# Zero products spread ahead of and between the first block's steps, and the two experts' weights computed behind the picks, in a two-part transformer kernel

## The reference

```python
def _hier_moe(h, w_group, b_group, w_expert, b_expert, w_gate, w_up, w_down):
    g_prob = jax.nn.softmax(hf @ w_group, axis=-1)
    g_sel = jnp.argmax(g_prob + b_group, axis=-1)
    g_w = jnp.take_along_axis(g_prob, g_sel[:, None], axis=-1)
    e_logits = (hf @ w_expert).reshape(T, MOE_GROUPS, MOE_EXPERTS_PER_GROUP)
    e_prob = jax.nn.softmax(jnp.take_along_axis(e_logits, g_sel[:, None, None], axis=1)[:, 0], axis=-1)
    ...
    _, top_idx = lax.top_k(e_prob + e_bias, MOE_TOP_K)
    top_w = jnp.take_along_axis(e_prob, top_idx, axis=-1)
    top_w = top_w / jnp.sum(top_w, axis=-1, keepdims=True) * g_w
    ...
    def expert_block(args):
        xb, e = args
        return (jax.nn.silu(xb @ w_gate[e]) * (xb @ w_up[e])) @ w_down[e]
    ...
    return jax.ops.segment_sum(yp[dest] * w_s[:, None], tok_s, num_segments=T)
```

## Time and profile before

| | |
|---|---|
| median of three runs | 2360.21 us (2356.59 to 2367.82) |
| the profiled execution's own time | 2359.6 us |
| its span, from the first to the last instruction | 2357.8 us |
| PE busy | 2065.4 us (88%) |
| DVE busy | 1169.1 us (50%) |
| ACT busy | 824.2 us (35%) |
| MoE 0: logits kept by DVE, to the end of its last block | 241.3 to about 693 us |
| MoE 1: logits kept by DVE | 816.9 us |
| mean granted PE clock | 0.948 |

### The profile page before, as it was taken

The page is one execution under the profiler, slowest core; times in us unless marked ns, Lnnn a source line. Parts: engine busy times, 40 slices in busy tenths (PEclk is TensorE's granted clock), DMA queues, the critical chain, the costliest instruction groups (busy, mean ns, idle before and its releaser), DMA issues.

```text
span 2357.8 us, 47090 instructions
## 1 busy us (share of the span) xinstructions
PE 2065.4 (88%) x17804; PEld 1568.1 (67%) x17805; DVE 1169.1 (50%) x2331; ACT 824.2 (35%) x1618; POOL 25.9 (1%) x40
## 2 busy tenths in 40 slices
PE   7999888677779988676678999989999999999997
PEld 3567555344449855343445888877887888877886
DVE  4677422111126632111115666766667766766666
ACT  2232211011125411111114554545555554545554
POOL 0000000000000000000000000000001000100001
PEclk9999999888889999888899999999999999999999
DMA  9978799999996689999998645353555546343552
GB/s 392 339 289 350 325 430 431 431 431 431 431 421 249 236 360 431 431 431 431 431 431 339 202 139 184 108 175 111 169 153 195 183 151 207 108 142 109 197 154 79
DMA packets 273333, 662.59 MB, mean 281 GB/s; under 512 B 6065, under 2 KB 200625, under 8 KB 248113
## 3 DMA queue, kind: packets, MB, share of 16 engines
q1 hardware_dynamic: 273056, 658.82, 72.0%
q10 hardware_dynamic: 144, 2.03, 0.2%
HBM read 659.78 MB, written 1.05 MB: 280 GB/s over the span
## 4 chain that ended last, share of the span: by engine, by line
PE 68%; DMA 19%; DVE 5%; issue 3%; SPq 2%; ACT 1%; another core or an unknown queue 1%; DVEq 0%; ACTq 0%; PEldq 0%
PE ps L2178 20%; PE ps L2183 11%; DMA ring<-in_moe_w_up 8%; DMA A<-in_moe_w_up 8%; PE ps L1582 8%; PE ps L2452 4%; PE ps L1611 3%; DMA arena<-in_moe_w_up 2%; PE ps L2617 2%; PE ps L1564 2%; PE ps L1530 1%; PE ps L1981 1%; PE ps L1983 1%; PE ps L1982 1%; SPq L3007 1%
## 5 line engine op out<-in xcount | busy, mean ns | idle before, releaser
L2178 PE MATMUL ps<-XS,WS 128*128 128x512 f32 x1408 | 502.0, 401 | 8.4 <-DVE XS L691 7.5
L2163 DVE TENSOR_TENSOR WS<-ring,WS 128x1024 fp32r<-128x1024 f32 (+1 forms) x276 | 329.4, 1194 | 227.9 <-ACT WS L2158 227.3
L2158 ACT CAST WS<-ring 128x1024 fp32r<-128x1024 f32 (+1 forms) x276 | 282.8, 1025 | 331.5 <-PE ps L2183 314.1
L2183 PE MATMUL ps<-XS,WS 128*128 128x256 f32 x1408 | 396.2, 281 | 0.0
L1855 DVE TENSOR_TENSOR RS<-RS,ps 64x256 f32<-64x256 f32 x70 | 29.6, 423 | 595.2 <-ACT RS L1676 595.2
L2178 PEld LDWEIGHTS ps<-XS,WS 128*128 128x128 f32 x1408 | 266.6, 189 | 80.2 <-DVE XS L691 17.8
L1582 PE MATMUL ps<-ring,RS 128*32 128x256 f32 x2176 | 236.6, 446 | 86.0 <-DMA ring<-in_moe_w_up 31.8
L2183 PEld LDWEIGHTS ps<-XS,WS 128*128 128x128 f32 x1408 | 268.3, 191 | 0.2 <-issue 0.2
L1582 PEld LDWEIGHTS ps<-ring,RS 128*32 128x32 f32 x2176 | 125.5, 127 | 148.4 <-issue 126.7
L2178 PE MATMUL ps<-HS,WS 128*128 128x512 f32 x616 | 216.4, 396 | 0.0
L1582 PE MATMUL ps<-arena,RS 128*32 128x256 f32 x1120 | 163.2, 456 | 53.7 <-DMA A<-in_moe_w_up 27.5
(11 more groups left out here) (360 smaller groups left out, 3318.3 us busy)
## 6 DMA issues: line engine op xcount, KB each, us to landing
ring<-in_ffn_w_gu SPq DMA_DIRECT2D x90, 1024.0 KB, 7.5
arena<-in_moe_w_down SPq DMA_DIRECT2D x32, 2048.0 KB, 47.7
ring<-in_moe_w_up SPq DMA_DIRECT2D x32, 2048.0 KB, 46.4
ring<-in_moe_w_down SPq DMA_DIRECT2D x32, 2048.0 KB, 46.7
ring<-in_moe_w_gate SPq DMA_DIRECT2D x32, 2048.0 KB, 45.9
ring<-in_w_mod SPq DMA_DIRECT2D x24, 2048.0 KB, 11.9
ring<-in_ffn_w_down SPq DMA_DIRECT2D x32, 1408.0 KB, 6.5
SPARE<-in_moe_w_gate SPq DMA_DIRECT2D x16, 2048.0 KB, 43.2
```

The source lines that it names most:

```text
L2158: L.inc(L.eng.copy(self.parts(u)[0], source), self.w_high)
L2163: L.inc(L.eng.tensor_tensor(wl, self.unit(u)[1], high(wh), ALU.subtract), self.w_split)
L2178: L.eng.matmul(ps[:, bank, :].rearrange("p (j t) -> p j t", j=2), wh[:, i, :], moving[:, :, k, :], start=k == 0, stop=False)
L2183: mm = L.eng.matmul(ps[:, bank, 0:TL], wl[:, i, :], moving[:, 0, k, :], start=False, stop=k == total - 1)
```

## The change

The zero products are no longer in a row. Those of banks 1 and 4 stand ahead of PE's wait for `picks`, that of bank 5 stands behind `pick_block`, and that of bank 6 behind `turn_block`. The wait for the zeros themselves (`y_kept`, a memset by GpSimd) moves ahead of the first two. On DVE the eleven instructions of the weights `WT` move from ahead of the wait for `counts` to behind `picks`, the shift and `ranges`, just ahead of the twelve instructions for `places`. Nothing is added or taken out.

```diff
--- before.py
+++ after.py
@@ -1537,14 +1537,20 @@
                     mm.then_inc(self.block_turned.sem, 1)
 
                 zeros = self.YS.bitcast(BF16)
+
+                def clear(bank):
+                    pe.matmul(ps[:, bank, :], zeros[:, 0:P], zeros[:, 0:512], start=True, stop=False)
+
                 L.wait(self.rows_kept, NT)
+                pe.wait_ge(self.y_kept.sem, 1)
+                clear(1)
+                clear(4)
                 pe.wait_ge(self.picks.sem, 1)
                 pick_block()
-                pe.wait_ge(self.y_kept.sem, 1)
-                for bank in (1, 4, 5, 6):
-                    pe.matmul(ps[:, bank, :], zeros[:, 0:P], zeros[:, 0:512], start=True, stop=False)
+                clear(5)
                 pe.wait_ge(self.picked_kept.sem, 1)
                 turn_block()
+                clear(6)
 
                 for t in range(NT):
                     for c in range(2):
@@ -1767,14 +1773,6 @@
                 step(v.tensor_tensor(by_all(self.BOTH), of_group(self.CE), group4, ALU.mult), self.chosen)
                 for c in range(2):
                     L.inc(v.tensor_tensor(by_all(self.O32S[:, c]), of_group(self.OE[c]), group4, ALU.mult))
-                pick(self.GW, self.GP, self.OG, GROUPS)
-                for c in range(2):
-                    pick(self.WT[c], self.ES, self.OE[c], PER_GROUP)
-                step(v.tensor_tensor(self.WS, self.WT[0], self.WT[1], ALU.add))
-                step(v.reciprocal(self.WS, self.WS))
-                step(v.tensor_tensor(self.WS, self.WS, self.GW, ALU.mult))
-                for c in range(2):
-                    step(v.tensor_tensor(self.WT[c], self.WT[c], self.WS, ALU.mult))
 
                 L.wait(self.counts, 1)
                 over = self.CNT[0:EXPERTS, 0:limits]
@@ -1823,6 +1821,14 @@
                 pick_matched().then_inc(self.picks.sem, 1)
                 L.inc(shift())
                 L.inc(v.tensor_copy(self.FIRSTI, self.FIRST), self.ranges)
+                pick(self.GW, self.GP, self.OG, GROUPS)
+                for c in range(2):
+                    pick(self.WT[c], self.ES, self.OE[c], PER_GROUP)
+                step(v.tensor_tensor(self.WS, self.WT[0], self.WT[1], ALU.add))
+                step(v.reciprocal(self.WS, self.WS))
+                step(v.tensor_tensor(self.WS, self.WS, self.GW, ALU.mult))
+                for c in range(2):
+                    step(v.tensor_tensor(self.WT[c], self.WT[c], self.WS, ALU.mult))
 
                 def lane_of(ap, c, t):
                     return ap[:, NT * c + t:NT * c + t + 1]
```

## The result

The changed kernel takes 2365.05 us in the median of 22 runs (2354.45 to 2370.94), the kernel before 2358.56 us in 22 runs. The ratio is 1.0021 with a 95% interval of 1.0013 to 1.0029: 5 us slower by the ratio, on which this text goes, and 6.5 us by the two medians. That is within 0.5% as forecast, but on the other side of no change, and the median lies above the range that was given (up to 2364 us). The prediction held that 12 us would be needed to tell a change from none; with 22 runs each the interval is 4 us wide. The profiled execution has a span of 2366.6 us, before 2357.8.

What follows compares the result with a forecast made beforehand. The prediction took the DMA queue as full from the restart of the loads to each MoE stage's end. Gains of 1.2 and 1.5 us made 2360.2 - 2.7 = 2357.5 us, range 2357.5 less 6 and up to 2364.

Steps and rivals of the forecast that it cites:

- The weights off the path to the picks: DVE ahead of the picks: the counts' reader starts earlier, gaining 1.30 us in MoE 0 and 1.33 in MoE 1.
- The weights put back behind the picks: DVE between `ranges` and `places`: `places` and all behind come 0.89 us later in MoE 0, 0.86 in MoE 1.
- The zero products: PE ahead of the picks: two products fill the 0.71 us wait, exceed it by 0.22; picks start 1.08 us earlier.
- The step that failed: PE from picks through turn and table: first expert starts 1.4 us earlier in MoE 0, 1.9 in MoE 1.
- the slow rival: PE's clock stays low into the first expert because of short waits: about 2366 us; chance 0.07 for 2362 to 2366.
- the covering load: SP in MoE 1: load behind the table comes 1.5 us earlier, next issue falls inside that load's 4.9 us.
- The way through the full queue: DMA from the loads' restart to stage end: an earlier restart brings the end forward by as much.
- the first rival: Gain lost in the DMA-bound part, up to 2.7 us per stage: 2360 us; chance 0.16 for gain swallowed or halved.
- The sum: Both MoE stages: 1.2 us gained in MoE 0, 1.5 in MoE 1, together 2.7, from 1.8 to 3.5.

Runs made afterwards that it cites:

- second profile of the same kernel: The changed kernel run once more, with nothing altered, beside the kernel before: 2363.9 us, ratio 1.0012.
- extra pair of loads: Kernel before plus one more pair of register loads of the block bounds on PE, ahead of the expert loop: 2361.8 us, ratio 0.9999.
- three products: Changed kernel plus three products of zeros behind the block table on PE: 2359.33 us, ratio 1.0000.
- filled: Changed kernel plus eight products of zeros into PSUM bank 2 behind the block table on PE: 2357.58 us, ratio 0.9996.
- weights in waits: Changed kernel with the group's weight pick moved into the softmax's wait and two experts' picks ahead of the wait for counts: 2356.14 us, ratio 0.9995.
- weights behind alone: Kernel before with only DVE's weights moved behind the picks, the four zero products left in a row: 2361.0 us, ratio 1.0007.

## Why the prediction was wrong, point by point

**The weights off the path to the picks: right.** 1.30 us forecast, 1.34 measured, with a DVE wait of 0.77 us for the counts.

**The weights put back behind the picks: right as to DVE.** The last `places` came 0.87 us later, forecast 0.89; the table's copy and SP's load behind it 1.1 us earlier in MoE 0 (forecast 1.0) and 1.65 in MoE 1 (forecast 1.5).

**The zero products: right, and partly lucky.** The forecast had PE at the low clock there. In the first profile it was at the full clock, so the first two products took 0.59 us, all inside PE's wait, and the picks on PE started 1.43 us earlier, forecast 1.08. In the second profile of the same kernel, where the clock was low at that place, they started 1.26 us earlier.

**The step that failed** is the end of the next one: "One of them takes 1.32 / 4 = 0.33 us", and "The first expert starts at 259.9 us instead of 261.34". I took the end of the table on the array for the start of the expert, as the earlier trace rows show it before: 261.34 for both. What lies between the two in PE's instruction stream, the head of the loop, two register loads and their waits, was put at nothing. It stands in none of the rows that I had read: the timeline leaves the sequencer out, and the stream ran ahead of the array while that worked off the zero products and the turn. The rows by source line have it, from 258.9 to 261.1 us in the kernel before. With `places` the last thing to come, the stream waits there, and its own 2.65 us come behind it. Two numbers in the earlier trace rows would have raised the question: the last place before ended at 258.56 us, and the expert started 2.7 us later. The extra pair of loads (1.24 us, uncovered) shows that this was what counted. The forecast of 1.4 us earlier in MoE 0 became 0.8 later, and that of 1.9 us in MoE 1 became 0.1 later.

**The clock: the slow rival was right in effect and wrong in its cause.** I had it lose to short waits between the picks, the turn and the table. It lost to one idle stretch that the change itself opened between the table and the expert, which by the rows of before wasn't there. Its price in MoE 0: the first block 2.6 us longer (6.28 against 3.66 at the full clock), which with the start's 0.8 gives the 3.4 us of the restart. I had priced a longer low stretch at 5 us; it ended within the block. That the measured 2365 us lie at this rival's 2366 is luck: its 3.6 us for MoE 0 were 5 lost less 1.4 gained, where 2.6 and 0.8 were lost, and its 2 us for MoE 1 came as 1.7 and 0.1.

**MoE 1: the covering load did not cover.** I had the load behind the table, 1.5 us earlier, decide, and the next issue inside its 4.9 us. The next issue came 26.19 - 19.37 = 6.8 us later, 1.9 us too late. The 1.66 us gained are given back in this idle time: the last loads of MoE 1 are issued 0.24 us later after the logits than before, in the second profile 0.09.

**The way through the full queue: right, and the first rival with it.** What the restart loses, the last block of MoE 0 loses: it starts 408.2 to 408.6 us behind the restart in all ten profiles. But how long its 64 products take depends on how much of them meets the low clock, which differs by profile. In the kernel before they took 6.27 us. The chain of the kernel after, then of the one with three products:

```profile
689.13 6.19 PE ps L1588 x64
...
681.33 3.66 PE ps L1590 x64
```

The mean granted clock over these products is 0.57 before, 0.58 after and 1.00 with three products. They take 6.2 to 6.4 us in six of the ten (both of the kernel after among them), 5.35 in three (filled, weights in waits, one more pair of loads), and 3.66 with three products. So from the restart to the end of MoE 0 it takes 421.5 us before, 421.6 and 421.5 in the two profiles of the kernel after, and 418.8 with three products, 2.6 of these 2.7 us being the last block's clock. This is the first rival's term, up to 2.7 us for a stage in either direction. In MoE 0 it doesn't blur the comparison of before and after, since both have the slow last block.

In MoE 1 it does. The last blocks, before, after and after once more:

```profile
1251.07 5.03 PE ps L1582 x64
...
1258.42 6.56 PE ps L1588 x64
...
1253.59 5.00 PE ps L1588 x64
```

They start 434.20, 434.44 and 434.29 us after the logits. So of the 1.7 us that MoE 1 cost in the first profile, 1.5 are the clock in its last block (a mean of 0.55 against 0.72 before and in the second profile), and only 0.2 (in the second profile 0.1) came through the queue.

**The sum.** -1.2 and -1.5 us were forecast. To the end of the stages MoE 0 cost 3.5 and 3.6 us in the two profiles, MoE 1 1.7 and 0.1: together 5.2 and 3.7. To the start of the last blocks it is 3.8 and 3.6. Both agree with both ratios (5 us with 3.1 to 6.8, and 2.8 with 0.7 to 5.0).

**What is shown and what isn't.** Shown: that the start hangs on the last `places` plus 2.65 us, and that the clock fell in all seven stages in which PE was idle for 1.98 to 2.13 us ahead of the expert (four in the two profiles of the kernel after, two with the weights behind alone, one with the weights in the waits) and in none of the thirteen others, with 1.57 us or less. Filled with zeros that no one reads, the same kernel loses the slow first blocks, and its time (0.9984 to 1.0008) lies below the first measurement of the kernel after (1.0013 to 1.0029), though its interval overlaps with that of the second (1.0003 to 1.0021). Not shown: whether as long an idle time would do it behind work without a pause. In each of the seven the last product of the table had a pause of 0.12 to 0.16 us ahead of it, and no run has 2 us of idle time without one. Shown in the profiles, but not in time to more than the interval: how the cost splits between start and clock. The three-product kernel, as late but with its clock held, is at 1.0000 (0.9988 to 1.0012), so the start is worth less than 2.8 us. The kernel with the weights behind alone has the same first blocks, and its stages are as long as in the first profile of the kernel after (457.60 and 448.13 us), but its ratio is only 1.0007; its interval reaches to 1.0019 and overlaps with both of the kernel after, and nothing tells whether they differ.

## What to carry to other kernels

An engine's row starts when its array or pipe does, not when its stream gets there. Ahead of a loop with register loads, ask what the stream still has to do behind its last wait, look for it in the sequencer's rows of those source lines, and count from that wait, not from the end of the work before. A step that is moved off a path and put behind another wait has a second reader: here the last `places` had none of the slack that DVE's later wait of 1.88 us seemed to promise, since that wait was for PE's work and not the other way round. And where work of no use is moved ahead into a wait, look at what it covered where it stood. When two profiles of a stage differ, compare the start of its last block before its end: here the end carries up to 2.7 us of the clock's chance.

## What the runs showed of the hardware that I had not expected

The way of PE's stream from a wait through the loop's branch and two register loads to the first product took 2.5 to 2.7 us in this kernel, and one more pair of register loads 1.24 us. The timeline and the chain book it as "issue", or show nothing of it where it runs behind work that is queued. The Trainium skill ("DMA: Bandwidth & Descriptors", Latency and other measured facts) gives a floor of about 600 ns for one `tensor_load`. By that a pair takes 1.2 us at least, as an estimate from the page's figure, which comes near the 1.24 us measured and would have given half of the 2.65 us that the prediction left out. The rows of the loads themselves don't bear the floor out: they have 0.32 and 0.50 us in MoE 0, and the two of the kernel before in MoE 1 have 0.30 each. Only with the register operations behind it does a load come to 0.6 us and more.

TensorE's clock fell to 1.2 GHz while PE was idle from 263.58 to 265.71 us (1.00 in the window from 261 to 264, a mean of 0.65 over the idle time, 0.50 from 267 to 270), behind a table with a pause of 0.16 us ahead of each of its last products. With 0.65 us of products of zeros between the two it stayed at 2.4 GHz, in both stages. The Trainium skill ("TensorE: Matmul & The Clock Gate", Part 1) says that the moment of such a change isn't tied to the kernel's start. The first blocks agree only in part: they took 6.28, 6.44 and 6.50 us in MoE 0, and 5.21, 5.26 and 5.27 in MoE 1, closer together in each stage than between the two.
